# Expert picks of a routed feed-forward stage: VectorE's tables moved to PSUM, digit loops turned, turning points and first gates moved to other tiles

## The reference, cut to what matters

```python
q = (xc @ w_q).reshape(-1, 8, 2, 64)                      # 8 heads, two half queries
s = einsum('thpd,pkd->thpk', q, sub_keys)                 # 128 keys per half
sv, si = top_k(s, 16)                                     # 16 best per head and half
cand = sv[:, :, 0, :, None] + sv[:, :, 1, None, :]        # 16 x 16 sums per head
cand_id = si[:, :, 0, :, None] * 128 + si[:, :, 1, None, :]
cv, ci = top_k(cand, 16)                                  # 16 best sums per head
eid = take_along_axis(cand_id, ci); g = softmax(cv)       # experts and their shares
a = gelu(xc . u[eid]); out = sum(g * a * v[eid])
```

## Time and profile before

| | |
|---|---|
| three runs | 3337.12, 3339.4, 3341.34 us; median 3339.4 us |
| profiled execution, first to last instruction | 3335.1 us |
| median less the span | 4.3 us |
| busy, share of the span | PE 97%, PEld 86%, DVE 72%, ACT 50%, POOL 15% |
| chain that ended last | PE 83%, DVE 10%, DMA 2%, ACT 2%, issue 2% |
| mean granted TensorE clock | 0.989 of full speed |
| `u` tiles 0 to 63 | from 221.2 us (layer 0) and 1269.6 us (layer 1) |

### The profile page before, as it was taken

How to read it: one execution, slowest core, us unless ns; L and a number is a source line. 1 busy time by engine, 2 the same in 40 slices (tenths; PEclk the granted TensorE clock), 3 DMA queues, 4 the chain that set the end, 5 groups by cost and what they waited for, 6 DMA issues and landing times.

```text
span 3335.1 us, 57375 instructions
## 1 busy us (share of the span) xinstructions
PE 3218.4 (97%) x22739; PEld 2871.8 (86%) x22739; DVE 2410.0 (72%) x4140; ACT 1665.9 (50%) x2679; POOL 503.8 (15%) x363
## 2 busy tenths in 40 slices
PE   6999999999999889999999999999999999999999
PEld 6789887889898669987789999989879999888798
DVE  7879999777667559899966556558775555687754
ACT  3454555444454464455544445446554444565543
POOL 1169100000000258600000000001240000022300
PEclk9899999999999999999999999999999999999999
DMA  8445455577766225545566665555345555544355
GB/s 330 159 134 183 130 158 167 189 252 240 244 213 243 83 65 165 158 134 169 170 195 219 190 187 170 184 182 169 114 132 172 184 179 184 173 149 138 124 183 168
DMA packets 160537, 582.27 MB, mean 175 GB/s; under 512 B 18449, under 2 KB 20241, under 8 KB 160145
## 3 DMA queue, kind: packets, MB, share of 16 engines
q1 hardware_dynamic: 156528, 569.69, 53.4%
q10 hardware_dynamic: 3168, 8.35, 0.7%
q0 software_dynamic: 576, 0.57, 0.1%
HBM read 576.96 MB, written 1.05 MB: 173 GB/s over the span
## 4 chain that ended last, share of the span: by engine, by line
PE 83%; DVE 10%; DMA 2%; ACT 2%; issue 2%; POOL 1%; ACTq 0%; DVEq 0%; POOLq 0%
PE P L806 22%; PE P L1997 20%; PE P L1974 19%; PE P L857 11%; PE P L1960 2%; DVE LOW L521 1%; DVE ssd_a L2790 1%; PE P L786 1%; DMA RING<-in_pv 1%; DMA RING<-in_pu 1%; PE P L824 1%; PE P L882 1%; ACT HI L508 1%; PE P L1053 1%; PE P L789 1%
## 5 line engine op out<-in xcount | busy, mean ns | idle before, releaser
L521 DVE TENSOR_TENSOR LOW<-RING,HI 128x1024 fp32r<-128x1024 f32 x882 | 1073.4, 1227 | 382.9 <-ACT HI L508 382.1
L508 ACT ACTIVATE HI<-RING 128x1024 fp32r<-128x1024 f32 x988 | 1035.6, 1053 | 374.7 <-DMA RING<-in_pu 153.3
L806 PE MATMUL P<-HTH,HI 128*128 128x256 f32 x2240 | 324.6, 288 | 9.1 <-DVE ssd_a L2824 4.8
L806 PE MATMUL P<-HTH,LOW 128*128 128x256 f32 x2240 | 318.5, 285 | 7.5 <-DVE LOW L521 7.5
L806 PE MATMUL P<-HTL,HI 128*128 128x256 f32 x2240 | 316.7, 284 | 0.0
L806 PEld LDWEIGHTS P<-HTH,HI 128*128 128x128 f32 x2240 | 291.1, 193 | 20.0 <-issue 7.8
L1974 PE MATMUL P<-HTH,HI 128*128 128x256 f32 x2048 | 300.4, 287 | 6.0 <-DVE peer_eq L2233 3.6
L806 PEld LDWEIGHTS P<-HTH,LOW 128*128 128x128 f32 x2240 | 291.1, 193 | 10.6 <-DVE LOW L521 10.6
L1974 PEld LDWEIGHTS P<-HTH,HI 128*128 128x128 f32 x2048 | 274.9, 191 | 20.0 <-issue 6.7
L806 PEld LDWEIGHTS P<-HTL,HI 128*128 128x128 f32 x2240 | 291.2, 193 | 0.0
L1974 PE MATMUL P<-HTL,HI 128*128 128x256 f32 x2048 | 290.9, 285 | 0.0
(11 more groups left out here) (436 smaller groups left out, 5134.5 us busy)
## 6 DMA issues: line engine op xcount, KB each, us to landing
RING<-in_pu SPq DMA_DIRECT2D x256, 512.0 KB, 3.6
RING<-in_pv SPq DMA_DIRECT2D x256, 512.0 KB, 3.6
RING<-in_ada SPq DMA_DIRECT2D x64, 512.0 KB, 4.7
RING<-in_fgA SPq DMA_DIRECT2D x44, 512.0 KB, 4.3
RING<-in_fuA SPq DMA_DIRECT2D x44, 512.0 KB, 4.3
RING<-in_fdA SPq DMA_DIRECT2D x44, 512.0 KB, 4.3
RING<-in_fgB SPq DMA_DIRECT2D x44, 512.0 KB, 3.6
RING<-in_fuB SPq DMA_DIRECT2D x44, 512.0 KB, 3.6
```

What stands on the lines that cost most here:

```text
L508: act.activation(c.his[i % NHL], c.raw[m % NR], ACT.Copy).then_inc(*c.hi.at(("hi", m)))
L521: eng.tensor_tensor(c.low[m % NR], c.raw[m % NR], c.his[i % NHL].bitcast(F32), ALU.subtract).then_inc(*sig.at(("lo", m)))
L806: m = pe.matmul(ps[:, 0:256], w[:, k * 128:k * 128 + 128], c.ht[h][:, k, :], start=i == 0 and k == 0, stop=i == 2 and k == 7)
```

## The change

The tables `sf`, `ca`, `cb`, `cu` and a new one, `second` (the second half's values), are put into PSUM banks 0 and 1 (`c.y[0]`, `c.y[1]`), as fp32 words. The look-up's axes become (k, h, a) with the digit `a` innermost, so that the sum reads neighbours; `heads16` shrinks to 16 numbers. `peer_parts` writes the low part directly instead of by way of `rest`. The two products of a gate become one over both parts, for which `parts` is laid out anew. ACT's exponentials move to tiles 22 and 39, PE's turns to tiles 29 and 40, the early gates begin at tile 43, and POOL makes LOW up to tile 43. The bank of the first turn is held until the second turn. Two orderings are added: the tables wait for the norm's readers, and `v` tile 0 waits for the tables' last reader.

```diff
-EXP_T, FIRST_T, SECOND_T = 28, 34, 44
+EXP_T, FIRST_T, SECOND_T = (22, 39), 29, 40
+GATES_T, POOL_T = 43, 43
...
-        order = [((f"pq{l}", j), "pool") for j in range(8)] + [((f"pu{l}", j), "pool" if j <= SECOND_T else "dve") for j in range(64)]
+        order = [((f"pq{l}", j), "pool") for j in range(8)] + [((f"pu{l}", j), "pool" if j <= POOL_T else "dve") for j in range(64)]
...
-        self.eq = [at(2048 * q, 1024).bitcast(F16).rearrange("p (a k h) -> p a k h", a=16, k=16) for q in range(2)]
-        self.si, self.sv, self.sf = at(10240, 512).bitcast(U32), at(10752, 512), at(11264, 256).bitcast(F16)
+        self.eq = [at(2048 * q, 1024).bitcast(F16).rearrange("p (k h a) -> p k h a", k=16, h=8) for q in range(2)]
+        self.si, self.sv = at(10240, 512).bitcast(U32), at(10752, 512)
+        self.sf, self.ca, self.cb = c.y[0][:, 0:256], c.y[0][:, 256:384], c.y[0][:, 384:512]
+        self.second, self.cu = c.y[1][:, 0:128], c.y[1][:, 128:256].bitcast(U32)
...
-        self.ca, self.cb = at(12288, 128).bitcast(F16), at(12544, 128).bitcast(F16)
-        self.cu = at(12800, 256).bitcast(U32)
...
+        self.parts = g2[:, :].rearrange("p (g q t) -> p g q t", q=2, t=8)
...
+        self.shares = [pc[:, 1024 * h:1024 * h + 1024].rearrange("p (q b n t) -> p q b n t", q=2, b=8 // SIDE, t=SIDE)
+                       for h in range(2)]
...
-    n = 62 - SECOND_T
-    return range(32 * (j - SECOND_T - 1) // n, 32 * (j - SECOND_T) // n) if SECOND_T < j < 63 else range(0)
+    n = 63 - GATES_T
+    return range(32 * (j - GATES_T) // n, 32 * (j - GATES_T + 1) // n) if GATES_T <= j < 63 else range(0)
...
-                ps = open_bank(pe, c, s, "picks_turned", t)
+                ps = open_bank(pe, c, s, "picks_turned", t, held=True)
...
+                if t:
+                    leave_bank(c, s, "picks_turned", 0)
+                    leave_bank(c, s, "picks_turned", 1)
+    for q in range(2):
+        c.y_last[q] = s + "route"
...
-            if j == (EXP_T, SECOND_T)[t]:
+            if j == EXP_T[t]:
...
-    sf = f.sf[:, 256 * t:256 * t + 256]
     dve.wait_ge(*c.dve.last())
-    dve.tensor_copy(sf.rearrange("p (q a h) -> p h q a", q=2, a=16), si.rearrange("p (h q) a -> p h q a", q=2))
     sv4 = sv.rearrange("p (h q) k -> p h q k", q=2)
+    second = f.second.rearrange("p (h k) -> p h k", h=8)
+    if t == 0:
+        for q in range(2):
+            dve.wait_ge(*c.by("y_free", s + "norm", q))
+    dve.tensor_copy(second, sv4[:, :, 1, :]).then_inc(*c.dve.at())
+    dve.tensor_copy(f.sf.rearrange("p (q h a) -> p h q a", q=2, a=16),
+                    si.rearrange("p (h q) a -> p h q a", q=2)).then_inc(*c.dve.at((s, "tables", t)))
     cd = f.sb[t]
+    dve.wait_ge(*c.by(s, "tables", t))
...
-                      sv4[:, :, 1, :].unsqueeze(2).broadcast_to([128, 8, 16, 16]), ALU.add).then_inc(*c.dve.at())
+                      second.unsqueeze(2).broadcast_to([128, 8, 16, 16]), ALU.add).then_inc(*c.dve.at())
...
+    turned = f.cu.rearrange("p (h k) -> p k h", h=8)
...
-    dve.tensor_scalar(cut, cit, 4, None, ALU.logical_shift_right).then_inc(*c.dve.at())
+    dve.tensor_scalar(f.cu, cit, 4, None, ALU.logical_shift_right).then_inc(*c.dve.at())
...
-    dve.tensor_copy(ca.rearrange("p (k h) -> p k h", h=8), turned).then_inc(*c.dve.at())
+    dve.tensor_copy(f.ca.rearrange("p (k h) -> p k h", h=8), turned).then_inc(*c.dve.at())
...
-    for q, (src, dst) in enumerate(((ca, f.ei), (cb, f.ej))):
+    for q, (src, dst) in enumerate(((f.ca, f.ei), (f.cb, f.ej))):
         eq = f.eq[q]
-        dve.tensor_tensor(eq, src.rearrange("p (k h) -> p k h", h=8).unsqueeze(1).broadcast_to([128, 16, 16, 8]),
-                          f.heads16.unsqueeze(2).broadcast_to([128, 16, 16, 8]), ALU.is_equal).then_inc(
+        dve.tensor_tensor(eq, src.rearrange("p (k h) -> p k h", h=8).unsqueeze(3).broadcast_to([128, 16, 8, 16]),
+                          f.heads16.unsqueeze(1).unsqueeze(1).broadcast_to([128, 16, 8, 16]), ALU.is_equal).then_inc(
...
-        dve.tensor_tensor(eq, eq, sf[:, 128 * q:128 * q + 128].rearrange("p (a h) -> p a h", h=8).unsqueeze(
-            2).broadcast_to([128, 16, 16, 8]), ALU.mult).then_inc(*c.dve.at())
+        dve.tensor_tensor(eq, eq, f.sf[:, 128 * q:128 * q + 128].rearrange("p (h a) -> p h a", h=8).unsqueeze(
+            1).broadcast_to([128, 16, 8, 16]), ALU.mult).then_inc(
+            *c.dve.at(*([("y_free", s + "route", n) for n in range(2)] if t and q else [])))
         dve.wait_ge(*c.dve.last())
-        dve.tensor_reduce(dst[:, 128 * t:128 * t + 128].rearrange("p (h k) -> p k h", h=8),
-                          eq.rearrange("p a k h -> p k h a"), AX.X, ALU.add).then_inc(*c.dve.at())
+        dve.tensor_reduce(dst[:, 128 * t:128 * t + 128].rearrange("p (h k) -> p k h", h=8), eq, AX.X,
+                          ALU.add).then_inc(*c.dve.at())
...
-    share, rest = ps[:, 256:384], f.rest
-    high, low = (f.parts[:, q, 128 * t:128 * t + 128] for q in range(2))
+    share = ps[:, 256:384].rearrange("p (g t) -> p g t", t=8)
+    high, low = (f.parts[:, 16 * t:16 * t + 16, q, :] for q in range(2))
...
-    dve.scalar_tensor_tensor(out=rest, in0=share, scalar=SHARE, in1=high, op0=ALU.mult, op1=ALU.subtract).then_inc(
-        *c.dve.at(("free", s, "picks_turned", t)))
-    dve.wait_ge(*c.dve.last())
-    dve.tensor_copy(low, rest).then_inc(*c.dve.at((s, "parts", t)))
+    dve.scalar_tensor_tensor(out=low, in0=share, scalar=SHARE, in1=high, op0=ALU.mult, op1=ALU.subtract).then_inc(
+        *c.dve.at(("free", s, "picks_turned", t), (s, "parts", t)))
...
-    for q in range(2):
-        m = dve.tensor_tensor(f.share[b][q], f.is_col, tokens(f.parts[:, q, :], 64), ALU.mult)
-    m.then_inc(*c.dve.at((s, "picks", part, g)))
+    parts = f.parts[:, g, :, :].rearrange("p q (b t) -> p q b t", b=n)
+    dve.tensor_tensor(f.shares[b], f.is_col.unsqueeze(1).broadcast_to([128, 2, n, 64, SIDE]),
+                      parts.unsqueeze(3).broadcast_to([128, 2, n, 64, SIDE]), ALU.mult).then_inc(
+        *c.dve.at((s, "picks", part, g)))
...
-    feed(dve, c, "dve", f.u, SECOND_T)
...
-    for j in range(SECOND_T + 1, 64):
+    for j in range(GATES_T, 64):
```

More of the change, by code:

```diff
@@ L1910, in __init__ @@
         self.row, self.col = ij[:, 0:256], ij[:, 256:512]
-        self.parts = g2[:, :].rearrange("p (q t) -> p q t", q=2)
+        self.parts = g2[:, :].rearrange("p (g q t) -> p g q t", q=2, t=8)
         self.iota = c.arena[s, "iota"][:, :].rearrange("p (n t) -> p n t", t=SIDE)
-        self.heads16 = c.arena[s, "iota16"][:, :].rearrange("p (a h) -> p a h", a=16)
+        self.heads16 = c.arena[s, "iota16"][:, 0:16]
         self.is_col = c.arena[s, "eq"][:, :].rearrange("p (b n t) -> p b n t", b=8 // SIDE, t=SIDE)
-        self.rest = c.arena[s, "eq"][:, 0:256].bitcast(F32)
         self.is_row = [oh[:, 1024 * b:1024 * b + 1024].rearrange("p (b n t) -> p b n t", b=8 // SIDE, t=SIDE)
                        for b in range(2)]
+        self.shares = [pc[:, 1024 * h:1024 * h + 1024].rearrange("p (q b n t) -> p q b n t", q=2, b=8 // SIDE, t=SIDE)
+                       for h in range(2)]
         self.share = [[pc[:, 512 * b:512 * b + 512].rearrange("p (b n t) -> p b n t", b=8 // SIDE, t=SIDE)
@@ L2104, in peer_scalar @@
     act.activation(f.iota, c.const("iota").unsqueeze(2).broadcast_to([128, 128, SIDE]), ACT.Copy)
-    act.activation(f.heads16, c.const("iota")[:, 0:16].unsqueeze(2).broadcast_to([128, 16, 8]), ACT.Copy).then_inc(
+    act.activation(f.heads16, c.const("iota")[:, 0:16], ACT.Copy).then_inc(
         *c.act.at((s, "iota")))
@@ L2180, in peer_experts @@
         peer_parts(dve, c, f, 0)
-    cit, cut = f.ci[:, 128 * t:128 * t + 128], f.cu[:, 128 * t:128 * t + 128]
-    ca, cb = f.ca[:, 128 * t:128 * t + 128], f.cb[:, 128 * t:128 * t + 128]
+    cit = f.ci[:, 128 * t:128 * t + 128]
+    turned = f.cu.rearrange("p (h k) -> p k h", h=8)
     dve.wait_ge(*c.dve.last())
-    dve.tensor_scalar(cut, cit, 4, None, ALU.logical_shift_right).then_inc(*c.dve.at())
+    dve.tensor_scalar(f.cu, cit, 4, None, ALU.logical_shift_right).then_inc(*c.dve.at())
     dve.wait_ge(*c.dve.last())
-    turned = cut.rearrange("p (h k) -> p k h", h=8)
@@ L2187, in peer_experts @@
-    dve.tensor_copy(ca.rearrange("p (k h) -> p k h", h=8), turned).then_inc(*c.dve.at())
+    dve.tensor_copy(f.ca.rearrange("p (k h) -> p k h", h=8), turned).then_inc(*c.dve.at())
     dve.wait_ge(*c.dve.last())
-    dve.tensor_scalar(cut, cit, 15, None, ALU.bitwise_and).then_inc(*c.dve.at())
+    dve.tensor_scalar(f.cu, cit, 15, None, ALU.bitwise_and).then_inc(*c.dve.at())
     dve.wait_ge(*c.dve.last())
-    dve.tensor_copy(cb.rearrange("p (k h) -> p k h", h=8), turned).then_inc(*c.dve.at())
+    dve.tensor_copy(f.cb.rearrange("p (k h) -> p k h", h=8), turned).then_inc(*c.dve.at())
```

## The result

The changed kernel took 3310.7 us (median of 4), the kernel before 3338.3 us (4 runs), ratio 0.9918, 95% interval 0.9906 to 0.9931. A second measurement of the same program gave 3314.0 us, ratio 0.9933, 0.9916 to 0.995. All 8 runs of it have a median of 3312.9 us, all 49 runs of the kernel before that stand beside this result and the experiments 3336.5 us (3330.7 to 3345.6): 23.6 us faster. Forecast were 20.0 us and 3319.4 us, with a range down to 3315 us.

The account below looks back on a forecast made before the run. PE was taken as the bound, losing 11.1 and 12.5 us in the two layers, mostly waiting for DVE; with 1.8 us left in each, 9.3 + 10.7 = 20.0 us are gained, 3339.4 to 3319.4 us, range 3315 to 3329 us.

Parts of the forecast that it names:

- What bounds the kernel, and the losses: PE, busy 97%; beside the `u` tiles it loses 11.1 us in layer 0, 12.5 in layer 1, to waits and slow clock.
- DVE's path: DVE's expert search, step by step with PSUM tables; shifted sums of t = 1 done at 337.7 us in layer 0.
- The turn: PE's second turn, after tile 40: its wait of 3.07 us becomes 0.2 us, DVE having 1.3 us to spare.
- The losses left: Per layer: 0.2 us at the turn, 0.3 bad luck with POOL, 0.4 first gate, 0.9 ACT's copies; 1.8 us.
- undisturbed work: PE from `u` tile 0 to tile 63's last block: tiles 183.4 us, 32 gates 20.6, turns about 0.5; 204.5 us.
- The 0.9 us "for ACT": PE's waits on ACT's copies in the stage changed, 0.9 us, kept among the losses left in each layer.
- The forecast's own sum: DVE's pace against PE's over 20 tiles of early gates: DVE 74.4 us, PE 78.2 us, so DVE follows.
- The baseline: Median before the change, 3339.4 us, taken as 4.3 us above the profiled span of 3335.1 us.
- (a): DVE gains less, the look-up's sum staying at 3.95 us; gain 6 us, 3333 us; chance 0.22.
- (b): Slower than before: PSUM serves the table patterns at two steps an element; 3366 us; chance 0.07.
- (c): PSUM does not avoid DVE's waits for POOL, any SBUF use being excluded; 3340 us, no change; chance 0.07.
- (d): PE gains all, DVE even quicker than forecast; 3316 us; chance 0.07.

Follow-up runs that it names:

- e3: Changed kernel with its fp32 tables in SBUF instead of PSUM, axes and all else the same; 3352.8 us, ratio 1.0052.
- e4: Changed kernel with the look-up's digit axis outermost as before, so the sum reads with a stride, tables still in PSUM; 3322.7 us, ratio 0.9951.
- e7: Changed kernel with each of the look-up's four sums done twice, 9.2 us more DVE work by the shares of t = 1; 3323.2 us, ratio 0.9964.
- e8: Changed kernel with the look-up's two sums done twice for t = 1 only, 4.6 us more DVE work; 3321.0 us, ratio 0.9949.
- e11: Changed kernel with the second exponential after tile 40, the tile of the turn, instead of 39; 3321.0 us.
- e1: Changed kernel's PSUM tables, turned axes and single product, but the earlier kernel's tiles for exponentials, turns, gates and POOL, no held bank; 3327.4 us, ratio 0.9979.
- e2: Kernel before with the changed kernel's tiles for exponentials, turns, gates, POOL and held bank; SBUF tables, old axes, two products kept; 3338.0 us, ratio 1.0004.
- e5: Changed kernel with the gate's two parts as two products again; 3309.2 us.
- e9: Changed kernel with the early gates from tile 45 as before instead of 43, LOW unchanged; 3311.4 us.
- e6: Changed kernel with the bank of the first turn given back at once instead of held; 3323.9 us, ratio 0.9963.

## Why the prediction was too small

- **What bounds the kernel, and the losses.** Right. The most that could be had was put at 23.6 us; the stretches gave 24.0 us.
- **DVE's path.** Right nearly to the digit: add, compare, product and sum forecast at 2.30 (the sum 2.29), measured 2.29 us; shifted sums of t = 1 done at 336.5 us, or 117.0 us after the first `u` matmul, forecast 337.7 - 221.2 = 116.5. `e3` shows that the place does it, `e4` that the axes add their own part.
- **The turn.** Right: 0.2 us, but with less to spare than the 1.3 us forecast: 0.5 to 0.6 us (`e4`, `e7`, `e8`). `e11` and `e1` confirm that the old 3.1 us were the order of the exponential, not DVE.
- **The losses left, "0.2 + 0.3 + 0.4 + 0.9 (ACT) = 1.8 us".** This term failed: only the 0.2 us is there, in each layer. Against 204.5 us put down for undisturbed work, it took 204.3 us to the last block of tile 63 (the block begins at 423.85), with 0.2 us of waiting in it. The 0.3 and 0.4 us were averages over bad luck with POOL. DVE did stand beside POOL, 1.3 us at the shifted sums (334.92) and 2.2 us at the first gate's product (341.69), and was in time for PE both times. The 1.6 us too much make 3.2 us in both layers, and 0.4 us a layer that the undisturbed work was put too high make the 4.0 us between 20.0 and 24.0.
- **The 0.9 us "for ACT" were waits for DVE.** The earlier trace rows names ACT's copy because it ended last before PE went on. In the kernel before, the four small waits of each layer all end 0.15 us after the end of DVE's product for that gate, the same 0.15 us as at the first gate; in layer 1 the trace names DVE itself for the first of them. For the gate at 395.07 (rows of the kernel before, below) the product ends at 394.92. ACT's copy that ends at 395.07 belongs to the gate just before it, and the bank that PE takes there had been copied out at 390.91.

```profile
394.17 0.75 DVE L2260 TENSOR_TENSOR peer_pc<-peer_eq,peer_g 128x512 f16<-128x512 f16 x2
...
395.07 0.64 PE L1960 MATMUL P<-peer_pc,ACC 128*128 128x64 f16 x16 [0.17 <-ACT peer_a L2056]
```

The forecast's own sum shows it when it is done for the 18 tiles of before: 18 LOW, 18 gates before a LOW and 14 before a gate are 74.7 us of DVE, against 18 x 2.88 + 20.6 = 72.4 us of PE, an estimate from the earlier trace rows. DVE fell behind. The single product takes 2.2 us off, and the two tiles more give PE 5.8 us and DVE 1.9 us of work, so either should do. Behind the first gate, the product ended at least 0.48 us before PE took it in `e1` (old tiles, one product), 1.02 us in `e2` (20 tiles, two products), 0.29 us in `e5` and 0.39 us in `e9`. The forecast took over a wait that its own change removed twice over.
- **The baseline.** The 3339.4 us were a median of three runs and 2.9 us above the median of all 49. 3336.5 - 24.0 = 3312.5 us, against 3312.9 for all 8 runs: the stretches alone explain the time. The 3310.7 us of the first four runs are 2.2 us lower still, which is spread. With the stretches forecast right, 3339.4 - 24.0 = 3315.4 us would have been just inside the range. The profiled run after had 3311.66 us for a span of 3309.9, 1.8 us around it; I had put 4.3 us there by subtracting a span from a median of other runs.
- **The range.** Its low end lay 24.4 us below a baseline that was itself 3 us high. It held the terms of the sum and no allowance for the spread of the stages that the change does not touch.
- **The rivals.** (a) did not occur, and `e4` prices it at 6 us a layer and not the 7 I gave it. (b) and (c) fell with the 2.29 us. (d), all of the gain, is what came about.
- **The page's rules.** The Trainium skill's larger fixed part from PSUM ("VectorE: DVE Perf Modes", the section on the TRN2 errata) was not seen. With one operand in PSUM 2048 elements took 2.29 us, and the sum, all in SBUF, took 2.29 us too. The Trainium skill's rule on who excludes whom ("SBUF — State Buffer", "Who interferes with whom") has VectorE and GpSimd exclude each other for a second SBUF input or a two-port copy, and not for a sum. It agrees with `e3` in each row above.

## What to carry to other kernels

Moving the second operand of VectorE's work to PSUM buys back the waits for GpSimd, but it turns into time only where the order of the work asks for the result earlier; tables alone gave a third of it, the order alone nothing, both 24 us. Do not take the engine that a wait is put down to at its word: look which instruction ended just before each such wait. Before crediting a faster engine, look which instruction the late one really stands behind (here an exponential queued behind a tile's gelu). Take the baseline from as many runs as can be had, and measure a local change by its own stretch.

## What the hardware showed that I had not expected

- A wait of 2.9 to 5.3 us of PE cost 1.4 to 2.6 us more in slow clock afterwards (`e11` 2.9 and 1.5; `e8` 3.0 and 1.4; `e4` 3.5 and 2.6; `e6` 4.6 and 2.4; `e7` 5.3 and 2.1), and `e2`'s of 11.4 us, in another kernel, 2.3 us. These are waits beyond the 0.2 us of the changed kernel. The clock adds 40 to 75% to a wait of 3 to 5 us and 20% to one of 11 us.
- Stages without any edit moved by up to 6.7 us between programs (256.8 to 263.5 us, the mixing stage between the layers), where PE ran at the lower level for 17.1 us in `e5`, the shortest, and 34.1 us in `e8`, the longest; the stretch of the changed kernel repeats to 0.1 us.
- A copy or cast of VectorE into PSUM took 0.42 us for 256 numbers and 0.30 us for 128. The same two into SBUF, where they did not stand for GpSimd, took 0.29 and 0.23 us (`e3`, at 314.13 and 313.99). So PSUM cost the small copies about 0.1 us each and spared them waits of 2.0 and 2.2 us (`e3`, at 229.41 and 231.59).
